# Two hybrid decoder layers on one core: new order of the expert weights' units, one weight row in four unsplit, 8 KB pieces

## The reference

```python
def hier_moe(x, norm_w, wg, bg, we, be, w_gate, w_up, w_down):
    h = rms_norm(x, norm_w).reshape(-1, D)
    g_p, g_idx = lax.top_k(g_prob, 1)              # one of 4 groups
    e_p, e_idx = lax.top_k(softmax(e_logits), 2)   # two of its 4 experts
    ...
    for e in range(N_EXPERTS):                     # 16 experts
        a = jax.nn.silu(h @ w_gate[e]) * (h @ w_up[e])   # 2048 -> 512
        y = y + combine[:, e:e + 1] * (a @ w_down[e])    # 512 -> 2048
    return x + y
```

## Time and profile before

| | |
|---|---|
| median of 3 runs | 1600.03 us (1599.61 to 1603.97) |
| the profiled execution | 1598.73 us |
| its span in the trace | 1596.9 us |
| mean granted TensorE clock | 0.987 |
| TensorE, VectorE, ScalarE busy | 95%, 79%, 62% of the span |
| DMA | 471.53 MB, 295 GB/s over the span |

### The profile page before, as it was taken

How to read it: one execution, slowest core, us unless ns; L and a number is a source line. 1 busy time by engine, 2 the same in 40 slices (tenths; PEclk the granted TensorE clock), 3 DMA queues, 4 the chain that set the end, 5 groups by cost and what they waited for, 6 DMA issues and landing times.

```text
span 1596.9 us, 20533 instructions
## 1 busy us (share of the span) xinstructions
PE 1517.5 (95%) x6622; PEld 1091.2 (68%) x6622; DVE 1255.6 (79%) x1677; ACT 983.4 (62%) x1294; POOL 12.1 (1%) x23
## 2 busy tenths in 40 slices
PE   8999899998999999999999999899999999999998
PEld 8997894676666666666666667666666666666665
DVE  4898989756879688697978856788878869787884
ACT  5444342354768577576757754576767756776772
POOL 0000100000000000000000000000000000000000
PEclk9999999999999999999999999999999999999999
DMA  8973542443899899999989983289989999998993
GB/s 235 368 238 126 175 142 81 157 166 128 323 335 394 320 356 388 365 335 371 397 320 362 400 329 106 80 322 347 395 321 352 396 361 337 370 393 322 364 400 135
DMA packets 159755, 471.53 MB, mean 295 GB/s; under 512 B 20922, under 2 KB 40844, under 8 KB 159284
## 3 DMA queue, kind: packets, MB, share of 16 engines
q1 hardware_dynamic: 158148, 466.85, 79.1%
q10 hardware_dynamic: 1520, 3.59, 0.6%
HBM read 468.30 MB, written 4.21 MB: 296 GB/s over the span
## 4 chain that ended last, share of the span: by engine, by line
PE 70%; DVE 17%; issue 7%; ACT 5%; DMA 1%; SPq 0%; DVEq 0%; ACTq 0%
PE ps L2332 14%; DVE split_lo L1187 11%; PE ps L2299 10%; PE ps L1941 8%; PE ps L1943 8%; PE ps L1942 8%; PE ps L2300 7%; PE ps L2316 4%; PE ps L2022 3%; ACT split_hi L743 2%; PE ps L2248 1%; PE ps L2352 1%; ACT cat L743 1%; PE ps L1887 1%; PE ps L1922 1%
## 5 line engine op out<-in xcount | busy, mean ns | idle before, releaser
L1187 DVE TENSOR_TENSOR split_lo<-ring,split_hi 128x1024 fp32r<-128x1024 f32 x732 | 856.4, 1212 | 195.0 <-ACT split_hi L743 189.6
L743 ACT ACTIVATE split_hi<-ring 128x1024 fp32r<-128x1024 f32 x732 | 747.3, 1053 | 331.0 <-PE ps L1943 254.7
L2299 PE MATMUL ps<-split_hi,cat 128*128 128x512 f32 x1024 | 437.9, 428 | 50.8 <-DVE split_lo L1187 50.5
L2300 PE MATMUL ps<-split_lo,cat 128*128 128x512 f32 x1024 | 407.6, 398 | 0.0
L2299 PEld LDWEIGHTS ps<-split_hi,cat 128*128 128x128 f32 x1024 | 194.4, 190 | 190.6 <-DVE split_lo L1187 144.4
L2332 PE MATMUL ps<-ring,work 128*128 128x512 f32 x512 | 230.1, 592 | 0.0
L2300 PEld LDWEIGHTS ps<-split_lo,cat 128*128 128x128 f32 x1024 | 195.7, 191 | 30.1
L1941 PE MATMUL ps<-split_hi,cat 128*128 128x512 f32 (+1 forms) x464 | 205.7, 443 | 3.9 <-DVE cat L1187 3.8
L1943 PE MATMUL ps<-split_hi,cat 128*128 128x512 f32 (+1 forms) x464 | 179.9, 388 | 0.0
L1942 PE MATMUL ps<-split_lo,cat 128*128 128x512 f32 (+1 forms) x464 | 179.4, 387 | 0.0
L2332 PEld LDWEIGHTS ps<-ring,work 128*128 128x128 f32 x512 | 96.9, 189 | 97.4 <-issue 91.9
(11 more groups left out here) (237 smaller groups left out, 1186.3 us busy)
## 6 DMA issues: line engine op xcount, KB each, us to landing
ring<-in_w_gate SPq DMA_DIRECT2D x128, 1024.0 KB, 6.6
ring<-in_w_up SPq DMA_DIRECT2D x128, 1024.0 KB, 7.1
ring<-in_w_down SPq DMA_DIRECT2D x128, 1024.0 KB, 7.0
ring<-in_w_in_e SPq DMA_DIRECT2D x16, 1024.0 KB, 7.5
ring<-in_w_out_e SPq DMA_DIRECT2D x16, 1024.0 KB, 5.2
ring<-in_w_in_e SPq DMA_DIRECT2D x30, 512.0 KB, 5.1
ring<-in_pool_w_o SPq DMA_DIRECT2D x4, 1024.0 KB, 10.1
ring<-in_w_in_e SPq DMA_DIRECT2D x12, 256.0 KB, 6.1
```

What stands on the lines that cost most here:

```text
L743: return nc.scalar.activation(out, in_, ACT.Copy, scale=scale)
L1187: return tt(dst, full, hi.bitcast(F32), ALU.subtract)
L2299: mm(ps[:, bank, :], tokens, hi[:, k, :], start=q == 0 and k == 0, stop=False)
L2300: last = mm(ps[:, bank, :], tokens, lo[:, k, :], start=False, stop=q == 7 and k == 1)
```

## The change

- The unit lists: before the first pass g0 alone (FIRST); a pass that another follows (MID) is u0 g1 d0 u1 g2 d1 u2 g3 d2 u3 g0' d3, where g0' is the next pass's first gate matrix (EPG, "g"); the last pass (LAST) is u0 g1 d0 u1 g2 d1 u2 g3 u3 d2 d3.
- In a down half, of four weight rows one is read unsplit instead of two: the order is split, split, unsplit, split. A down matrix has 6 split units instead of 4, a MID pass 88 instead of 80. The blocks with an unsplit row are now given back by `used`. `plain_used` is gone.
- `down` waits for both parts of the turned product (`actT_out`) at its start; before, the unsplit rows, which came first, needed only the first copy.
- Gate and up blocks: one piece of four neighbouring weight rows per partition (8 KB) instead of two pieces of two rows (4 KB each); the token order follows (r = 4), in `x_block` and `gain_perm`.
- `choose_slots` of the next pass moves from beside u0 to d3; its transposes become `turn_pick`, beside `turn_act(0)`. `turn_act(3)` moves from d2 to g0'. `later_rounds` moves from between units 35 and 36 (in g2) to after unit 40 (in d1). `times_up` stands one unit earlier against its `turn_act`.

```diff
-UNITS = [(0, "g"), (0, "u"), (1, "g"), (0, "d"), (1, "u"), (2, "g"), (1, "d"), (2, "u"), (3, "g"), (3, "u"),
-         (2, "d"), (3, "d")]
+FIRST = [(0, "g")]
+EARLY = [(0, "u"), (1, "g"), (0, "d"), (1, "u"), (2, "g"), (1, "d"), (2, "u"), (3, "g")]
+MID = EARLY + [(2, "d"), (3, "u"), (EPG, "g"), (3, "d")]
+LAST = EARLY + [(3, "u"), (2, "d"), (3, "d")]
...
+def split_units(order, j):
+
+    return 1 if order[j // 4][1] == "d" and j % 2 else 2
+
+
...
-            return x_part(part, t, 4 * n, 512).rearrange("p (c r s) -> p c r s", c=2, r=2)
+            return x_part(part, t, 4 * n, 512).rearrange("p (r s) -> p r s", r=4)
 
         def x_block(t, n):
-            return x_sb[:, t, n * 512:(n + 1) * 512].rearrange("p (c s r) -> p c r s", c=2, r=2)
+            return x_sb[:, t, n * 512:(n + 1) * 512].rearrange("p (s r) -> p r s", r=4)
...
-        actT = [cat_cut(2 * D + i * HALF, 2, P) for i in range(2)]
+        actT = [cat_cut(2 * D + i * HALF, 3, P) for i in range(2)]
...
-            w = a[name][l].rearrange("e (c p r) n -> p e c (r n)", p=P, r=2)
-            return w[:, bass.ds(g * EPG + e, 1), 2 * (j % 4):2 * (j % 4) + 2, :]
+            w = a[name][l].rearrange("e (c p r) n -> p e c (r n)", p=P, r=4)
+            return w[:, bass.ds(g * EPG + e, 1), j % 4:j % 4 + 1, :]
...
+        def wait_released(eng, l, p, order, j, first=0):
+
+            u = units_before(order, j + 1)
+            if split_units(order, j) == 1:
+                wait_used(eng, l, p, first * PASS_UNITS + u)
             else:
-                eng.wait_ge(moe[l]["lo"], p * PASS_UNITS + (first * PASS_UNITS + 2 * (SPLIT_BLOCKS.index(j) + 1)))
+                eng.wait_ge(moe[l]["lo"], unit_at(p, first * PASS_UNITS + u))
...
-                        copy(actT32[e % 2], rows[:, 2:4, :]).then_inc(m["actT_hi"], 1)
-                        copy(actT[e % 2][0], rows[:, 0:2, :]).then_inc(m["actT_hi"], 1)
+                        copy(actT[e % 2][0], rows[:, 0:3, :]).then_inc(m["actT_hi"], 1)
+                        copy(actT32[:, e % 2, :], rows[:, 3, :]).then_inc(m["actT_hi"], 1)
...
-                        split(p, 0, 4)
+                        split(p, 0, 1)
+                        gate(p, 0)
+                        split(p, 1, 4)
                         y_lo(p - 1, 0)
-                        split(p, 4, 7)
+                        split(p, 4, 6)
                         y_lo(p - 1, 1)
-                        split(p, 7, 8)
+                        split(p, 6, 8)
                         add_y(p - 1, 0)
                         split(p, 8, 11)
                         add_y(p - 1, 1)
                         split(p, 11, 12)
                         add_y(p - 1, 2)
-                        split(p, 12, 16)
+                        split(p, 12, 13)
+                    times_up(0, 13)
+                    split(p, 13, 15)
+                    if not first_pass:
                         add_y(p - 1, 3)
-                        split(p, 16, 19)
-                        gate(0)
-                        split(p, 19, 22)
-                    times_up(0, 22)
-                    split(p, 22, 26)
+                    split(p, 15, 18)
                     turned_lo(0)
-                    split(p, 26, 28)
+                    split(p, 18, 23)
+                    gate(p, 1)
+                    split(p, 23, 24)
                     slots_lo(p, 2)
-                    split(p, 28, 29)
-                    gate(1)
-                    split(p, 29, 30)
+                    split(p, 24, 28)
                     if not last_pass:
                         window_rows(p + 1)
-                    split(p, 30, 31)
+                    split(p, 28, 30)
...
+                    split(p, 30, 35)
+                    times_up(1, 35)
+                    split(p, 35, 40)
+                    turned_lo(1)
+                    split(p, 40, 41)
                     if first_pass:
                         later_rounds()
-                    split(p, 36, 42)
-                    times_up(1, 42)
-                    split(p, 42, 46)
-                    turned_lo(1)
-                    split(p, 46, 48)
+                    split(p, 41, 45)
+                    gate(p, 2)
+                    split(p, 45, 46)
                     slots_lo(p, 3)
-                    split(p, 48, 49)
-                    gate(2)
-                    split(p, 49, 62)
-                    times_up(2, 62)
-                    split(p, 62, 66)
+                    split(p, 46, 57)
+                    times_up(2, 57)
...
+                    split(p, 57, 62)
                     turned_lo(2)
-                    split(p, 66, 67)
-                    if not last_pass:
-                        if first_pass:
-                            dve.wait_ge(m["route_done"], 1)
-                        slots_lo(p + 1, 0)
-                    split(p, 67, 71)
-                    gate(3)
-                    split(p, 71, 76)
-                    if not last_pass:
-                        slots_lo(p + 1, 1)
-                    times_up(3, 76)
-                    split(p, 76, 78)
+                    split(p, 62, 67)
+                    gate(p, 3)
+                    split(p, 67, 68)
+                    if first_pass:
+                        dve.wait_ge(m["route_done"], 1)
+                    slots_lo(p + 1, 0)
+                    split(p, 68, 79)
+                    times_up(3, 79)
+                    split(p, 79, 84)
                     turned_lo(3)
-                    split(p, 78, 80)
-                    if last_pass:
-                        y_lo(p, 0)
+                    split(p, 84, 86)
+                    slots_lo(p + 1, 1)
+                    split(p, 86, 88)
...
-                    def down(e, between=lambda n: None):
-
-                        pe.wait_ge(m["actT_hi"], p * (2 * EPG) + (2 * e + 1))
...
+                    def turn_pick():
+
+                        for t in range(NT):
+                            last = turn(ps[:, BANK_P, t * P:(t + 1) * P], pick[:, t, :])
+                        last.then_inc(m["misc_done"], 1)
+
+                    def down(e, order, between=lambda n: None):
+
+                        pe.wait_ge(m["actT_out"], p * EPG + (e + 1))
                         for half in range(2):
-                            between(3 * half)
-                            j = 4 * UNITS.index((e, "d")) + 2 * half + 1
-                            wait_landed(pe, l, p, j)
-                            for h in range(2):
-                                w = raw_half(moe_slot(l, j), h).rearrange("p (n c) -> p n c", n=2)
+                            if e == 0 and not first_pass:
+                                pe.wait_ge(m["x_moved"], p * 4 + (2 * half - 1))
+                            banks = [ps[:, BANK_Y + 2 * half + n, :] for n in range(2)]
+                            for k in (0, 1, 3, 2):
+                                if k == 3:
+                                    j = 4 * order.index((e, "d")) + 2 * half + 1
+                                    wait_landed(pe, l, p, j)
+                                    w = raw_half(moe_slot(l, j), 1).rearrange("p (n c) -> p n c", n=2)
+                                    for n in range(2):
+                                        mm(banks[n], actT32[:, e % 2, :], w[:, n, :], start=False, stop=False)
+                                    continue
+                                between(3 * half + k)
+                                w = weights(2, 512)
                                 for n in range(2):
-                                    last = mm(ps[:, BANK_Y + 2 * half + n, :], actT32[e % 2][:, h, :], w[:, n, :],
-                                              start=e == 0 and h == 0, stop=False)
-                            last.then_inc(m["plain_used"], 1)
-                            for k in range(2):
-                                between(3 * half + 1 + k)
-                                w = weights(2, 512)
-                                pe.wait_ge(m["actT_out"], p * EPG + (e + 1))
-                                for n in range(2):
-                                    last = product(ps[:, BANK_Y + 2 * half + n, :], pick_parts(actT[e % 2], ALL, k),
-                                                   pick_parts(w, ALL, n), False, e == EPG - 1 and k == 1)
+                                    last = product(banks[n], pick_parts(actT[e % 2], ALL, k), pick_parts(w, ALL, n),
+                                                   e == 0 and k == 0, e == EPG - 1 and k == 2)
                                 last.then_inc(m["used"], 1)
...
+                    def beside_down3(n):
+
+                        if n == 1:
+                            choose_slots(p + 1)
                         if n == 2:
...
+                            fold(p, EPG, "g")
...
+                    down(2, MID, lambda n: fold(p, 3, "g") if n == 2 else None)
+                    project(3, "u")
```

(71 more changed lines are left out.)

383 lines of the change are left out of this document (194 added, 189 removed).

## The result

Slightly slower: 1608.33 us against 1600.03 (medians of 13 runs each), a ratio of 1.0047 with a 95% interval of 1.0036 to 1.0059. The forecast was 1588. The profiled execution after took 1606.55 us, 7.8 more than the one before; its span is 1604.5.

A forecast was written before the change was run, and what follows sets the result against it. TensorE was taken to bound the down units, VectorE the gate and up stretches. Terms -1.6 - 8.0 + 1.2 - 4.4 + 1.0 = -11.8 us from 1598.73 gave 1586.9, forecast 1588; range 1563 to 1612, the forecast's own 1576 to 1594.

The forecast's parts named there:

- the stretches: Gate and up work between down units: four stretches sum to 88.7 us against 87.1 before, buffer restarts costing what shorter bursts bring.
- four middle passes: Two MID passes per layer, each 139.1 us against 139.5: -1.6 us in all.
- two first passes: First pass of each layer: moving `later_rounds` out of u1 g2 saves 3.7 + 0.3 us per layer, -8.0.
- heads and token rows: Run's head: a split waits 0.6 us longer per layer, +1.2; token rows read every fourth number, +1.0.
- two last passes: Last pass of each layer: down units bring 2.8 us, earlier `times_up` costs 0.5 in u1 g2; -4.4 in all.
- Down units: TensorE's down units take 11.9 us instead of 12.6, one 14.7; the extra VectorE splits stay hidden, 9.9 of 11.9.
- Gate and up stretches: Middle pass's u0 g1, u1 g2, u2 g3, u3 g0' take 27.9, 21.4, 19.7, 19.7 us; VectorE sets the pace.
- 14.5 + 5.1 = 19.6, and `turned_lo` ends at 19.7: u2 g3 and u3 g0': VectorE reaches unit fourteen at 14.5 us, TensorE's remainder takes 5.1, low part ends at 19.7.
- Token rows, r = 4: Copies in the routing chain read every fourth number: nothing to 4.1 us, taken as 1.0.
- 8 KB pieces: Gate and up weight transfers: faster pieces bring nothing since no expert's copy waits; cost nothing, or 2 us if queue-bound.
- the down units start late: Rival, chance 0.20: TensorE waits 1.14 us in 28 of 32 down units, +32 us, 1620 us.
- The whole saving shows: Rival, chance 0.18: small steps fall into VectorE's idle time at stretch starts, 26 us more saved, 1562 us.

## Why the prediction was wrong, step by step

The step that failed is "the stretches". It costs the earlier `times_up` at its own 0.74 us, "no longer hidden behind TensorE's unit", and treats the gap as time alone. What TensorE's clock does after the gap was left out, though the earlier trace rows showed a stretch with a wait of TensorE that came out at 0.93. The gap brought nine falls of about 1.3 us; filling it alone, with useless work, took 11 us off by the ratios.

The terms, from the two profiled executions, against the sum of -11.8:

| term | forecast | measured | of it falls |
|---|---|---|---|
| four middle passes | -1.6 | +9.4 | +7.8 |
| two first passes | -8.0 | -3.5 | +3.9 |
| heads and token rows | +2.2 | +3.2 | not counted |
| two last passes | -4.4 | -1.3 | 0 |
| sum | -11.8 | +7.8 | +11.7 |

(The falls are counted at 1.3 us each, six and three; a pass is measured from the start of one d0 to that of the next; the row of the heads is all the rest of the run.) Without the falls the sum would be -3.9 us: the other 8 us are in the middle and last passes and the heads, as follows.

- *Down units, 11.9 us and 14.7:* right, 11.88 to 12.03, and 14.96. VectorE had 8.95 to 10.10 us of work in them where I counted 9.9, hidden as said.
- *Gate and up stretches, 27.9, 21.4, 19.7, 19.7:* right in size, 27.28, 21.82, 19.93, 19.92 where nothing falls; the pass 139.9 instead of 139.1. The step "14.5 + 5.1 = 19.6, and `turned_lo` ends at 19.7" even had both waits within 0.1 us of each other. I took the 19.7 as set by VectorE's work. VectorE does set the rhythm of the units, but 0.87 us of each of these three stretches came from where two small steps stand, and either alone keeps the stretch that long: with both moved, u2 g3 takes 19.06 us. The same sum without the 0.74 gives 13.8 + 5.1 = 18.9.
- *First passes:* `later_rounds` is hidden in d1 as said; -7.4 us without the falls.
- *Last passes:* mis-sized. I took 0.5 us for the early product in one stretch; it costs 0.88 in u1 g2 (19.94 after, 19.06 before) and 0.98 in u2 g3 u3 (29.10, 28.12), which uses up most of the 2.8 us of the downs.
- *Token rows, r = 4:* 1.0 us taken, and the path shows 0.4 in one layer. For the copies themselves I stood near the wrong end of my range: the one on VectorE went from 687 to 1073 ns, on ScalarE from 660 (with 4 KB pieces) to 1115. The rule of the Trainium skill (SBUF — State Buffer, Door 1: The DMA port swizzle), that moving to a new line of 16 bytes is penalised, is what the trace agrees with.
- *8 KB pieces, no cost and no gain:* right. ScalarE's copies waited 9.2 us for transfers, the mixer's alone, as before. The three stretches u1 g2, u2 g3 and u3 g0' moved 394 to 400 GB/s; the 358 of the Trainium skill (DMA: Bandwidth & Descriptors, Where 436 GB/s comes from) as a bound on reads from HBM did not bind after either.

Of the rivals, "the down units start late" named a wait that is there, but only at the six d0 after a u0 g1 (0.85 us each, 5.1 in all), where the forecast had counted it; at the other downs the gap before has already held TensorE back. The time came out in that rival's band (1605 and up) for another reason: 12 us of it are falls of the clock. "The whole saving shows" gave 1562; with both waits out the kernel takes 1565.8. I had made it depend on VectorE's idle time; it depended on the order of two steps.

Open: why the gap leads to a fall in some stretches and not in others of the same timeline (and likewise in the kernel before with the early product). The number is not fixed either: with 4 KB pieces the same gaps had six falls in the profiled execution instead of nine. In the heads the granted clock differs from run to run (0.80 to 0.96), and the kernels of the new order take 38.5 to 42.2 us there; that was not pursued.

## What to carry to other kernels

Where two waits end a stretch at nearly the same time, undoing one alone does not show its price; undo both before either is priced. A step pulled forward on one engine leaves a hole on the other: price the hole, and what TensorE's clock does after it. If it can't be closed by reordering, work that nobody needs, no longer than the hole, can close it, as it did here.

## What the hardware showed that was not expected

- After 0.69 to 0.82 us of idle time, one unit and then eight small matmuls (2.1 to 2.2 us in all), the granted clock of a stretch came out at 0.92 or 0.93 in nine stretches and at 1.00 in nineteen; two idle products in that place kept it at 1.00 in all 28.
- Reading every fourth 4-byte number from SBUF made a 128x512 copy 1.56 times (VectorE) and 1.69 times (ScalarE) as long as reading every second did.
